# Odd layer's q, k, v projection by seven products: the turns one product later, the squares behind both silus, the second tile's taps ahead of two additions

## The reference

```python
def _odd_mixer(x, w_in, conv_w, a_log, dt_bias, norm_w, w_out):
    hproj = x @ w_in
    qkv = jax.nn.silu(_causal_dwconv(hproj[..., :3 * GDN_W], conv_w))    # GDN_W = 1024, 4 taps
    gate = hproj[..., 3 * GDN_W:4 * GDN_W]
    ...
    q = _l2norm(_heads(qkv[..., :GDN_W], GDN_HEADS).astype(F32)) * (GDN_DK ** -0.5)
    k = _l2norm(_heads(qkv[..., GDN_W:2 * GDN_W], GDN_HEADS).astype(F32))
    v = _heads(qkv[..., 2 * GDN_W:], GDN_HEADS).astype(F32)
```

## Time and profile before

| | us |
|---|---|
| runs before, median of 3 | 3091.28 |
| lowest and highest of them | 3090.56, 3096.67 |
| the profiled execution, by its own clock outside | 3092.21 |
| its span in the trace | 3090.4 |
| PE busy in the span | 2853.5 (92%) |
| of it, the q, k, v projection, from the first turn to the last | 1603.15 to 1852.70 |

### The profile page before, as it was taken

One profiled execution on the slowest core, in us unless ns is written; L12 is line 12 of the kernel. 1 busy time (PEld: TensorE's weight loads), 2 busy tenths in 40 slices (PEclk: granted clock), 3 DMA queues, 4 the chain that ended last, 5 costly groups with the idle time before them and its releaser, 6 DMA issues. The chain is left out here.

```text
span 3090.4 us, 46057 instructions
## 1 busy us (share of the span) xinstructions
PE 2853.5 (92%) x17614; PEld 2401.6 (78%) x17614; DVE 1836.2 (59%) x2928; ACT 1216.8 (39%) x2134; POOL 393.4 (13%) x337
## 2 busy tenths in 40 slices
PE   8999967979899999999889889799987999999996
PEld 6888856878778888788777766699976888887885
DVE  4111125674679999736577772155538799996363
ACT  3211125752344444322355542355434444443221
POOL 0000046330200000000100001255412000000002
PEclk9999989989999999999999999899988999999998
DMA  4322243425222222444323322532032222224443
GB/s 166 101 89 95 68 152 112 132 68 177 102 77 96 82 82 82 164 159 143 126 97 109 129 90 77 168 98 98 16 137 97 82 82 82 85 86 179 144 143 126
DMA packets 150492, 339.69 MB, mean 110 GB/s; under 512 B 35952, under 2 KB 69936, under 8 KB 139696
## 3 DMA queue, kind: packets, MB, share of 16 engines
q1 hardware_dynamic: 120128, 299.52, 28.3%
q10 hardware_dynamic: 30192, 37.82, 3.5%
HBM read 252.17 MB, written 85.10 MB: 109 GB/s over the span
## 5 line engine op out<-in xcount | busy, mean ns | idle before, releaser
L308 PE MATMUL even_in_acc<-even_in_w_hi,even_x_hi 128*128 128x512 f32 x576 | 225.2, 391 | 13.8 <-DVE even_x_lo L266 13.8
L309 PE MATMUL even_in_acc<-even_in_w_lo,even_x_hi 128*128 128x512 f32 x576 | 224.9, 391 | 0.0
L310 PE MATMUL even_in_acc<-even_in_w_hi,even_x_lo 128*128 128x512 f32 x576 | 224.8, 390 | 0.0
L272 DVE TENSOR_TENSOR even_in_w_lo<-even_in_w_raw,even_in_w_hi 128x512 fp32r<-128x512 f32 x72 | 49.6, 691 | 291.9 <-ACT even_in_w_hi L229 291.9
L958 DVE TENSOR_TENSOR ffn_a_lo<-ffn_a_raw,ffn_a_hi 128x512 fp32r<-128x512 f32 x84 | 58.0, 691 | 232.5 <-ACT ffn_a_hi L879 232.5
L879 ACT CAST ffn_a_hi<-ffn_a_raw 128x512 fp32r<-128x512 f32 x84 | 52.3, 623 | 324.3 <-PE ffn_down_acc L921 303.9
L1041 POOL TENSOR_SCALAR ffn_down_rstd<-ffn_down_mean_var 128x1 f32<-128x1 f32 x16 | 6.0, 373 | 1350.3 <-DVE ffn_down_mean_var L976 1350.3
L308 PEld LDWEIGHTS even_in_acc<-even_in_w_hi,even_x_hi 128*128 128x128 f32 x576 | 108.6, 189 | 36.4 <-issue 13.8
L310 PEld LDWEIGHTS even_in_acc<-even_in_w_hi,even_x_lo 128*128 128x128 f32 x576 | 108.7, 189 | 22.8
L309 PEld LDWEIGHTS even_in_acc<-even_in_w_lo,even_x_hi 128*128 128x128 f32 x576 | 108.7, 189 | 22.5
L921 PE MATMUL ffn_down_acc<-two_hi,ffn_a_hi 128*128 128x512 f32 x352 | 109.2, 391 | 4.5 <-DVEq L952 2.6
(11 more groups left out here) (565 smaller groups left out, 8319.0 us busy)
## 6 DMA issues: line engine op xcount, KB each, us to landing
ffn_w_raw<-in_ffn_up SPq DMA_DIRECT2D x42, 1024.0 KB, 4.8
ffn_down_w_raw<-in_ffn_down SPq DMA_DIRECT2D x84, 512.0 KB, 3.6
ffn_a_raw<-hidden SPq DMA_DIRECT2D x88, 256.0 KB, 3.7
even_in_w_raw<-in_ev_w_in SPq DMA_DIRECT2D x18, 1024.0 KB, 5.7
hp<-even_in_stage ACTq DMA_DIRECT2D x18, 1024.0 KB, 4.2
even_out_w_raw<-in_ev_w_out SPq DMA_DIRECT2D x24, 512.0 KB, 3.5
hidden<-even_mixed SPq DMA_DIRECT2D x22, 512.0 KB, 2.6
ffn_w_raw<-in_od_w_qkv SPq DMA_DIRECT2D x11, 1024.0 KB, 5.7
```

What stands on the lines that cost most here:

```text
L272: dve.tensor_tensor(at(w_lo, k), w_raw[:, k], f32(at(w_hi, k)), ALU.subtract).then_inc(lo_ready, 1)
L308: pe.matmul(acc[:, h, t], xhi[:, k, tok], at(w_hi, k), start=(k == 0), stop=False)
L309: pe.matmul(acc[:, h, t], xhi[:, k, tok], at(w_lo, k), start=False, stop=False)
L310: mm = pe.matmul(acc[:, h, t], xlo[:, k, tok], at(w_hi, k), start=False, stop=(k == KD - 1))
```

## The change

Only orders are changed; each engine still issues the same instructions.

- PE: the first turn of each round stands after product 3 in place of product 2 (in round 0 it did before), the second after product 6 in place of product 5.
- ACT: both silus of a round stand ahead of both `take_rows`. The first `take_rows` follows split 4, the second moves out of the round into the start of the next one (`take_rows(tile - 1)`); split 1 stands ahead of the first silu and split 3 ahead of the second. In the last round the copy of the quarter of x stands ahead of the second silu.
- DVE: the other taps of the round's second tile stand ahead of `add_u4` and split 1. Split 4 stands between `add_c11` and `add_c12`. In the last round the split of the quarter of x stands ahead of `add_c11`.

```diff
                     product(m, i)
                     if m == 0 and i == 1:
                         turn_tile(1)
-                    if i == (3 if m == 0 else 2):
+                    if i == 3:
                         turn_tile(2 * m + 2)
-                    if i == 5:
+                    if i == 6:
                         turn_tile(2 * m + 3)
...
             for m in range(W):
                 more = m + 1 < W
                 tile = 2 * m + 2
+                if m > 0:
+                    take_rows(tile - 1)
                 keep_first(m)
...
                 if more:
                     split_hi(m + 1, 0)
+                    split_hi(m + 1, 1)
                 silu(tile)
                 if more:
-                    for i in range(1, 3):
-                        split_hi(m + 1, i)
-                take_rows(tile)
-                if more:
+                    split_hi(m + 1, 2)
                     split_hi(m + 1, 3)
-                silu(tile + 1)
-                if more:
-                    split_hi(m + 1, 4)
                 else:
                     act.wait_ge(quarter_in, 16)
                     act.wait_ge(prod_done, ORDER * m + 3)
                     act.copy(xhi[:, chunks[0], toks[1]], again).then_inc(quarter_hi, 1)
+                silu(tile + 1)
+                if more:
+                    split_hi(m + 1, 4)
+                take_rows(tile)
+                if more:
+                    split_hi(m + 1, 5)
+                else:
                     following.split_hi(act)
                 last_tap(m + PLAIN, 0)
                 if more:
-                    split_hi(m + 1, 5)
-                take_rows(tile + 1)
-                if more:
                     split_hi(m + 1, 6)
                 last_tap(m + PLAIN, 1)
+            take_rows(2 * LAST - 1)
...
                 add_u2(m)
                 if more:
                     split_lo(m + 1, 0)
+                other_taps(tile + 1)
                 add_u4(m)
                 if more:
                     split_lo(m + 1, 1)
-                other_taps(tile + 1)
                 add_c22(m)
                 add_u3(m)
                 if more:
                     split_lo(m + 1, 2)
                     split_lo(m + 1, 3)
-                add_c11(m)
-                add_c12(m)
-                if more:
-                    split_lo(m + 1, 4)
-                    split_lo(m + 1, 5)
                 else:
                     dve.wait_ge(quarter_hi, 1)
                     dve.tensor_tensor(xlo[:, chunks[0], toks[1]], again, f32(xhi[:, chunks[0], toks[1]]), ALU.subtract)
+                add_c11(m)
+                if more:
+                    split_lo(m + 1, 4)
+                add_c12(m)
+                if more:
+                    split_lo(m + 1, 5)
+                else:
                     following.split_lo(dve)
                 add_c21(m)
```

## The result

| us | before | now |
|---|---|---|
| median of 4 runs each | 3090.92 | 3060.7 |
| lowest and highest | 3086.85, 3096.67 | 3059.28, 3062.7 |
| profiled execution, its span | 3092.21, 3090.4 | 3061.42, 3059.6 |
| turn of tile 2 to turn of tile 22 | 232.28 | 202.98 |
| turn of tile 2 to the next step's first matmul | 245.14 | 215.82 |

The changed kernel takes 0.9901 of the time, 95% interval 0.9884 to 0.9919: 30.2 us less, where the sum of the prediction was 28.5.

What follows compares the result with a forecast made beforehand. A chain of taps (DVE), silu (ACT) and turn (PE) was taken as the bound; 23.75 + 2.83 - 0.1 + 0.93 + 1.1 = 28.5 us off the profiled 3092.21 gave 3063.7, range 3061 to 3074.

Steps and rivals of the forecast that it cites:

- The 23.75 us between turns 4 and 20: Gain claimed in the eight rounds between these turns: PE's waits, half-clock work and restarts, 23.75 us.
- Turn 4's 2.83: PE's wait ahead of the turn of tile 4 was to go: 2.83 us gained.
- Turn 2's 0.1: Round 0: split 1 ahead of the silu of tile 2 makes its turn late, a charge of 0.1 us.
- 0.93 + 1.1: Last round: 0.93 us from moving the turn of tile 21 behind product 6, 1.1 from an earlier `add_c21` on DVE.
- How the numbers follow: Closing step on the whole time: forecast chance 0.82, width 25.5 to 31.5 us, range 3061 to 3074.
- the full width of 31.5 us: Largest gain in the forecast's own width, 25.5 to 31.5 us, for clock falls, round 0 and the end.
- So does everything behind the block: Steps behind the projection were claimed to stay unchanged, since the next step starts from the block's end.
- A part stays: Rival: DVE or ACT keep a part of the wait in the rounds; 3072 us, chance 0.12.
- its 2.4: Time per round that DVE was said to have for its own waits: 18.5 us of work under 20.9.
- the copy's slack: In k rounds the turned tile's copy ends at 18.5, the second turn stands at 20.0: 1.5 us.
- The wait only moves: Rival: PE waits as long at the second turn or product 0; 3089 to 3095 us, chance 0.02.
- The load rival: Weight load behind the second silu becomes the bound beyond 10.9 us, gain eaten at 14.5; 3104 at 16, chance 0.04.

Runs made afterwards that it cites:

- load_late3: The changed kernel with three 64 KB loads put on SP's queue ahead of each weight load and waited for; 3095.42 us.
- rep_before: The kernel before, unchanged, profiled once more; span 3088.2 us, 242.40 us from the turn of tile 2 to the next step.

## Why the prediction was right, and where it missed

**The mechanism holds, step by step.** The 23.75 us between turns 4 and 20 came as 191.03 - 166.88 = 24.15: the rounds are 20.86 and not 20.91 long, 0.4 in eight. Turn 4's 2.83 came. Turn 2's 0.1 was paid, though no wait is shown: it comes 6.48 us behind turn 1, where it came 6.33 to 6.37 behind it in the four traces of before. The end gave 2.2 us in place of 0.93 + 1.1, though the two are not separate gains (1.56 for DVE's queue and 0.64 for the turn, none of it without DVE's part). To the next step the profiled executions differ by 29.3 us, where 28.5 were predicted: the term sizes are right to 0.8 us.

**The step that failed is "How the numbers follow", the base and the low end of the range.** The mechanism was right; what was mis-sized is the base from which the sum is taken off, and the width put around it. The forecast starts from one execution, 3092.21. That less the full width of 31.5 us is 3060.7, the measured median itself, and the low end was put at 3061. The prediction itself gives 3091.28 as the median of the runs; less the same 31.5 it is 3059.8, and the measured time lies inside. The runs showed a median of 3090.92, so 1.3 us of the 3.0 us by which the forecast missed are the base, and 1.7 are the gain, 30.2 in place of 28.5. The width held two falls of the clock, in the projection or in the idle stretches of later steps, and nothing else for the rest of the program, booked as unchanged: "So does everything behind the block". The rest of the program took 2836.9 to 2851.1 us in eight traces, a spread of 3.8 us in one kernel and 14.2 in the other. The spread of the runs of before, 3090.56 to 3096.67, was there to see and was taken only as a bound for what can be told from no change. A range of the same forecast with some 3 us more at the fast end would have held.

That the median came out on the wrong side by 0.3 us is luck: the profiled execution of the changed kernel, 3061.42, and the median of all seven runs, also 3061.42, lie inside the range. In the projection the mean gain is 27.6 us, so 2.6 of the 30.2 lie outside it. Their cause stays open. The means of the eight traces differ there by 2.2 us, which the 14 us of spread in the changed kernel doesn't tell from chance, nor does it rule out that the change passes on 1 or 2 us.

The slow side was wide for a rival that did not come: 3074.

**One execution of before is not its mean.** Its four falls were the most of four traces; the mean is 2.75. The gain read from it, 28.5, is 0.9 us above the 27.6 that the means give in the projection. The Trainium skill, "TensorE: Matmul & The Clock Gate", Part 1, says that the number of slow matmuls of one kernel differs from run to run, and it says so of a kernel's start. The table of repeats shows it in the middle of a program as well, with 2 to 4 falls. A fall measured 1.4 us, where the prediction's price was 1.5.

**The rivals.** "A part stays" did not come: DVE waits 0.21, 1.47 and 0.27 us in round 3, inside its 2.4, and the copy's slack is 1.5 as worked out. "The wait only moves" did not come; it is what happens without PE's part, at 1.2 us in four rounds. The load rival did not come, but its point was wrong by 2.6 us: it decides from 8.3 us behind the silu, not from 10.9. By the loop the gain is eaten at 8.3 + 28.5 / 8 = 11.9 us and not at 14.5, and `load_late3`, at 12.4, just beyond, took 3095.42. Its chance of 0.04 leant on a margin that was less than half as wide as it seemed, about 2 us and not 5.2.

## What to carry to other kernels

Where an in-order engine is made to wait by a chain, move the consumer later and take the foreign work out of the chain; here each alone left a wait in nearly every round. Size a slack inside a loop by the whole loop: a buffer that lies outside it pays once, not in each round. And build the range of a whole-program time from the spread of whole runs as well as from the edited stretch, and take it from the median of the runs and not from the one that was profiled.

## What the runs showed of the hardware

The same wait is followed by half clock in one execution and not in another. Ahead of tile 16 PE idled 3.12 us in before and 3.11 in its repeat; the turn, then the window behind it (clock is the third number from the end), of before and of `rep_before`:

```profile
1783.80 1.97 PE L2000 MATMUL odd_qkv_turn<-top_ident,even_mixed 128*128 128x128 f32 x8 [3.12 <-ACT even_mixed L2086]
...
1784.00:1786.00 2.00, 2.00 (x10) 1.90 (x10) 2.00 (x3) 0.97 (x3) 0.00 (x0) 0.50 0.00 0
```

```profile
1782.86 1.09 PE L2000 MATMUL odd_qkv_turn<-top_ident,even_mixed 128*128 128x128 f32 x8 [3.11 <-ACT even_mixed L2086]
...
1784.00:1786.00 2.00, 2.00 (x10) 1.64 (x9) 1.97 (x3) 1.01 (x1) 0.00 (x0) 1.00 0.01 4
```

Five waits of 2.8 to 3.1 us stand in each of the four traces of before, with 2 to 4 falls behind them. Behind the waits ahead of tiles 4 (2.83 to 2.85 us) and 10 (3.13 to 3.14) the clock fell in all four, behind that of tile 12 (3.08 to 3.09) in none, behind those of tiles 14 and 16 in one and two. A change that takes such waits away wins the falls too, and makes the stretch repeat to 0.05 us.
